# Adding the cross products of a blocked inversion on TensorE, with states and carries copied by ScalarE

## What is computed

```python
def rwkv_scan(state0, r, decay, k, v, a_neg, b, reverse, emit):
    def step(S, inp):
        r_t, w_t, k_t, v_t, a_t, b_t = inp
        sa = einsum('bhij,bhj->bhi', S, a_t)
        S = S * w_t[:, :, None, :] + sa[..., None] * b_t[:, :, None, :] + v_t[..., None] * k_t[:, :, None, :]
        y = einsum('bhij,bhj->bhi', S, r_t) if emit else None
        return S, y
    S, ys = lax.scan(step, state0, xs, reverse=reverse)
```

## Time and profile before

| | |
|---|---|
| runs, median | 1128.56 us (1125.03 to 1128.92, three runs) |
| profiled execution | 1121.17 us, span 1119.4 us |
| busy | TensorE 95%, weight loads 68%, VectorE 61%, ScalarE 35%, GpSimd 30% |
| chain that ended last | TensorE 79%, VectorE 13%, ScalarE 3%, DMA 2%, issue 2% |
| mean granted TensorE clock | 0.980 of full speed |

### The profile page before, as it was taken

The page is one execution under the profiler, slowest core; times in us unless marked ns, Lnnn a source line. Parts: engine busy times, 40 slices in busy tenths (PEclk is TensorE's granted clock), DMA queues, the critical chain, the costliest instruction groups (busy, mean ns, idle before and its releaser), DMA issues.

```text
span 1119.4 us, 17999 instructions
## 1 busy us (share of the span) xinstructions
PE 1063.4 (95%) x7147; PEld 765.1 (68%) x7147; DVE 685.8 (61%) x1456; ACT 396.8 (35%) x1000; POOL 341.4 (30%) x246
## 2 busy tenths in 40 slices
PE   4999999998897897999999999999999999999998
PEld 2544858766786585647559999844656469999743
DVE  3222315586998985697536555698696356555755
ACT  2212213675654141634223444310535114444200
POOL 0000100220021011162027888600251037888400
PEclk9999999998898898999999999999999999999999
DMA  9922342000002302734237544533642244554430
GB/s 354 317 76 76 136 150 80 1 1 1 2 2 86 114 23 76 259 117 151 76 101 231 168 152 163 210 117 112 226 143 83 76 151 151 165 188 176 153 111 37
DMA packets 96981, 140.22 MB, mean 125 GB/s; under 512 B 12255, under 2 KB 63106, under 8 KB 96770
## 3 DMA queue, kind: packets, MB, share of 16 engines
q1 hardware_dynamic: 96532, 138.94, 36.5%
q10 hardware_dynamic: 366, 0.13, 0.0%
HBM read 138.01 MB, written 1.05 MB: 124 GB/s over the span
## 4 chain that ended last, share of the span: by engine, by line
PE 79%; DVE 13%; ACT 3%; DMA 2%; issue 2%; SPq 0%; POOL 0%; DVEq 0%; ACTq 0%
PE bank L1420 22%; PE bank L1460 12%; PE bank L883 10%; PE bank L1231 8%; PE bank L1222 3%; PE bank L499 2%; PE bank L492 2%; DMA ring<-in_ada_w 2%; PE bank L1092 1%; PE bank L1265 1%; PE bank L1163 1%; PE bank L556 1%; PE bank L509 1%; DVE ring L2367 1%; PE bank L680 1%
## 5 line engine op out<-in xcount | busy, mean ns | idle before, releaser
L3089 POOL TENSOR_TENSOR small<-small,con 128x8 f32<-128x8 f32 (+4 forms) x23 | 32.5, 1418 | 423.1 <-DVE small L2741 130.7
L883 PE MATMUL bank<-work,ring 128*128 128x256 f32 (+1 forms) x368 | 118.4, 479 | 0.0
L883 PEld LDWEIGHTS bank<-work,ring 128*128 128x128 f32 x368 | 70.0, 193 | 44.0 <-issue 38.5
L2970 DVE SCALAR_TENSOR_TENSOR bank<-work,prm,bank 128x256 f32<-128x256 f32 x176 | 76.8, 482 | 1.1 <-ACT bank L2030 1.0
L1231 PE MATMUL bank<-ring,work 128*128 128x512 f32 (+1 forms) x192 | 71.7, 526 | 0.0
L2014 ACT ACTIVATE work<-bank 128x128 f32<-128x128 f32 x120 | 33.2, 276 | 103.2 <-PE bank L1420 100.6
L1420 PE MATMUL bank<-xc,work 128*128 128x128 f32 x512 | 65.9, 275 | 2.0 <-ACT work L2014 2.0
L1420 PE MATMUL bank<-work 128*128 128x128 f32 x512 | 65.7, 275 | 0.0
L1420 PEld LDWEIGHTS bank<-xc,work 128*128 128x128 f32 x512 | 61.5, 192 | 2.5 <-ACT work L2014 2.4
L1420 PEld LDWEIGHTS bank<-work 128*128 128x128 f32 x512 | 61.4, 192 | 0.0
L1420 PE MATMUL bank<-work,ring 128*128 128x128 f32 x448 | 59.2, 275 | 0.0
(11 more groups left out here) (526 smaller groups left out, 2291.3 us busy)
## 6 DMA issues: line engine op xcount, KB each, us to landing
ring<-in_w_up SPq DMA_DIRECT2D x32, 1024.0 KB, 7.7
ring<-in_w_in SPq DMA_DIRECT2D x24, 1024.0 KB, 9.1
ring<-in_w_down SPq DMA_DIRECT2D x16, 1024.0 KB, 6.1
ring<-in_ada_w SPq DMA_DIRECT2D x12, 1024.0 KB, 10.5
work<-in_w_up SPq DMA_DIRECT2D x12, 1024.0 KB, 7.0
ring<-in_w_out SPq DMA_DIRECT2D x10, 1024.0 KB, 7.4
work<-in_w_in SPq DMA_DIRECT2D x4, 1024.0 KB, 9.2
work<-in_w_down SPq DMA_DIRECT2D x4, 1024.0 KB, 6.2
```

Source lines behind the costliest of these rows:

```text
L883: ins = mm(b[0:rows, 0:toks], wt[:, k, off:off + rows], hT[:, k, 0:toks], start=(k == 0), stop=(k == KD - 1))
L2970: ins = STT(out=c, in0=hp[:, m % 2, half, tap:tap + SEQ], scalar=k2(l, "conv01", 1, 44 * tap + FB * half + m), in1=c, op0=MUL, op1=ADD)
L3089: return G.tensor_tensor(out_, in_, C("negpow", 1, rows).to_broadcast([rows, n]), POW)
```

## The change

For instances 0 to 3 the addition of the cross products moves from VectorE into PSUM. TensorE first multiplies the other half's right sides by an identity of 64 x 64 into the bank (two products of 512 columns, one per direction), waits on its own semaphore `cross_base` until they have landed, and then lets the eight cross products accumulate on them. ScalarE copies the sum to SBUF as it copies the other stages. `take_carry(2)` and `(3)`: TensorE adds the identity in PSUM, by one more product of 64 columns per head, and ScalarE copies the result. `take_state(0)` to `(3)`: VectorE only makes the gain, at steps 8, 10, 12 and 14; ScalarE copies the state, scaled, in four instructions of 64 columns each. All of VectorE's other asides in the second inversion go. Instances 4 to 7 keep VectorE's versions.

```diff
--- before.py
+++ after.py
@@ -177,6 +177,7 @@
 SEMAPHORES = """a_bar_sc act_T cc_zero column_sums first_consts hT_even hT_odd ssq_ctx angle angle_raw b_spread a_made bk_ch block_T bonus_in c0 c_masked cv_made c_silu c_tanh consts crow d_bias d_hat
  d_rstd d_var d_w decays derived dt_exp e_made ends g_tanh gelu_in gelu_tanh h0 hp_pads k_tok kk_rn kk_sq kkf
  lam_exp lam_sum lora lw_in k_rate maps_used m_bias mix_gmlp mix_rw mix_ssm mod_cols off_made off_step out_done p2_load pads pair_used
+ cross_base state_gain
  up_products up_copies up_corner x_sums weight_sums weight_step early_sums late_row_sums conv_made gelu_square
  params_1 params_2 q_tok qk_rot qk_rstd qk_sum qk_taken qk_turned qk_var r_ch r_grown rk_used rotated rotated_used row_sums rstd_1 rstd_f rstd_lat scale_a scanned row_inv
  sine ssq ssq_a ssq_f t64_diag turns_abs t_inv tables u_theta us v_centred var_1 var_a var_f vec_step vg_n vg_rstd vg_var weights_used
@@ -786,6 +787,12 @@
                     pe.wait_ge(*when_empty(("cross", i, g)))
                 pe.wait_ge(*turn((stage, i, g)))
                 b = bank_of((stage, i, g))
+                added = stage == "cross" and p == 0
+                if added:
+                    for d in range(2):
+                        rows = slice(64 * (1 - d), 64 * (1 - d) + 64)
+                        mm(b[rows, :], ident[rows, rows], factor(2 * i + d)[rows, 4 * g:4 * g + 4, :].rearrange("p a b -> p (a b)"), start=True, stop=False, skip_group_check=True).then_inc(S["cross_base"], 1)
+                    pe.wait_ge(S["cross_base"], 4 * i + 2 * g + 2)
                 for j in range(4):
                     m = 4 * g + j
                     for d in range(2):
@@ -796,7 +803,7 @@
                         if stage == "first":
                             ins = mm(b[one:one + 64, cols], t64[one:one + 64, inst, :], x[one:one + 64, :], start=True, stop=True)
                         elif stage == "cross":
-                            ins = mm(b[two:two + 64, cols], offs[p][one:one + 64, il, m, 32:96], x[one:one + 64, :], start=True, stop=True)
+                            ins = mm(b[two:two + 64, cols], offs[p][one:one + 64, il, m, 32:96], x[one:one + 64, :], start=not added, stop=True, skip_group_check=True)
                         else:
                             ins = mm(b[two:two + 64, cols], t64[two:two + 64, inst, :], x[two:two + 64, :], start=True, stop=True)
                 ins.then_inc(*filling((stage, i, g)))
@@ -813,7 +820,10 @@
                     b = bank_of(("carry", n))
                     for m in SIDES:
                         h, lo = head(m), 64 * (m // 4)
-                        ins = mm(b[lo:lo + 64, 64 * (m % 4):64 * (m % 4) + 64], x[:, m, 0:64], b_tok(n)[:, 64 * h:64 * h + 64], start=True, stop=True)
+                        o = b[lo:lo + 64, 64 * (m % 4):64 * (m % 4) + 64]
+                        ins = mm(o, x[:, m, 0:64], b_tok(n)[:, 64 * h:64 * h + 64], start=True, stop=(i > 1))
+                        if i == 1:
+                            ins = mm(o, ident[:, lo:lo + 64], ident[:, lo:lo + 64], start=False, stop=True)
                     ins.then_inc(*filling(("carry", n)))
                 pe.wait_ge(*turn(("st", n)))
                 b = bank_of(("st", n))
@@ -1793,16 +1803,35 @@
                     tanh_rows(n + 2)
                     key_rates(n + 2)
                 take_keyed_values(n)
-            for stage in ("first", "last"):
+            for stage in ("first", "cross", "last"):
                 for i in range(2):
                     for g in range(2):
                         take_solved(stage, i, g)
+
+            def take_state(n):
+                d = n % 2
+                act.wait_ge(S["state_gain"], n + 1)
+                act.wait_ge(*when_full(("st", n)))
+                b = bank_of(("st", n))
+                for j in range(4):
+                    ins = A.activation(state[:, d, j, :], b[:, 64 * j:64 * j + 64], ACT.Copy, scale=small[:, 288 + 4 * n + j:289 + 4 * n + j])
+                ins.then_inc(*emptying(("st", n)))
+
+            def take_carry(n):
+                act.wait_ge(*when_full(("carry", n)))
+                A.activation(carry[:, n % 2].rearrange("p j n -> p (j n)"), bank_of(("carry", n))[:, 0:256], ACT.Copy).then_inc(*emptying(("carry", n)))
+            take_state(0)
+            take_state(1)
+            take_carry(2)
+            take_carry(3)
             def take_early(j, t):
                 act.wait_ge(*when_full(("early", j, t)))
                 b = bank_of(("early", j, t))
                 A.activation(early_out[:, 2 * j + t, :], b[:, :], ACT.Copy).then_inc(*emptying(("early", j, t)))
             take_early(0, 0)
             take_early(0, 1)
+            take_state(2)
+            take_state(3)
             take_early(1, 0)
 
             def state_times(l):
@@ -2406,9 +2435,12 @@
                 b = bank_of(key)[:, 0:256].rearrange("p (j n) -> p j n", j=4)
                 TT(carry[:, n % 2], b, rep(C("ident64", 64), 4), ADD).then_inc(*emptying(key))
 
+            def state_gain(n):
+                return small[:, 288 + 4 * n:292 + 4 * n]
+
             def take_state(n):
                 d = n % 2
-                gain = small[:, 288 + 4 * n:292 + 4 * n]
+                gain = state_gain(n)
                 vec.wait_ge(S["ends"], n + 3)
                 TT(gain, outward(n), inward(n + 2), MUL).then_inc(S["vec_step"], 1)
                 vec.wait_ge(S["vec_step"], next(vec_steps))
@@ -2636,14 +2668,9 @@
 
             def states_between(step):
                 if step in (8, 10, 12, 14):
-                    q = (8, 10, 12, 14).index(step)
-                    add_cross(q // 2, q % 2)
-                if step in (27, 29):
-                    take_state((step - 27) // 2)
-                if step in (31, 33):
-                    take_carry(2 + (step - 31) // 2)
-                if step in (37, 38):
-                    take_state(step - 35)
+                    n = (8, 10, 12, 14).index(step)
+                    vec.wait_ge(S["ends"], n + 3)
+                    TT(state_gain(n), outward(n), inward(n + 2), MUL).then_inc(S["state_gain"], 1)
             invert(1, states_between)
             for k in range(RB):
                 ins = STT(out=bon[:, k, :], in0=kds[:, k, :], scalar=col("rk", 1, k), in1=rb[:, k, :], op0=MUL, op1=MUL)
```

## The result

The changed kernel takes 1119.47 us in the median of 18 runs (1113.25 to 1126.19), the kernel before 1127.01 us in 18 runs beside it. The ratio, taken over all runs, is 0.9943, with a 95% interval from 0.9922 to 0.9963: 6.4 us less, with an interval from 4.2 to 8.8 (the two medians alone lie 7.5 us apart). The forecast was 4.1 us less (0.9963), 1124.4 us in a range from 1119.5 to 1130.0. It was counted from the median of the first three runs, 1128.56; the ratio times that is 1122.1 us, inside the range, while the median of the 18 runs, 1119.47, stands right at its lower edge. A difference within 0.5% had been given 0.69 and a gain above that 0.24; the measured 0.57% is just on the side of the 0.24, and its interval covers both.

The account below looks back on a forecast made before the run. TensorE's queue was taken to bound the second join, VectorE level within 0.5 us. Projection 2.5 us earlier plus 1.6 us from full clock gave 4.1 us less: 1124.4 us, range 1119.5 to 1130.

Parts of the forecast that it names:

- The bound: At the second join TensorE's queue and VectorE's chain are level within 0.5 us, TensorE the later.
- the wait for state 0: Before the early projection TensorE waits 2.33 us for VectorE's `take_state(0)`, whose state sits in the projection's first PSUM bank.
- The cross stage: Cross solves of instances 0 to 3 on TensorE: 1.92 us each, issued by 364.04, lasts by 367.4.
- cross solve = 0.83 + 0.26 + 0.83: On TensorE: identity pair 0.83 us, wait for its own result 0.26, cross products 0.83; together 1.92.
- The bound below: In the cross stage an identity pair costs TensorE at least 0.83 us, since columns can't be skipped.
- ScalarE: Last copies end at 370.35; states take 0.31 us per 64 columns and leave their banks before the projection wants them.
- The projection: The early projection starts at 374.1 instead of 376.64; its first 16 rows take 7.1 us at full clock.
- The two terms of the sum: At the projection: 2.5 us from its earlier start and 1.6 us from full clock, together 4.1 us.
- The clock did not fall in the solves: Rival: eight short stops in the solves make the clock fall from the second cross on, 8.8 us slower, 1137.4; chance 0.06.
- The pairs overlap: Rival: identity pairs in the cross stage don't overlap, 3.3 us more, gain only 0.8 us, 1127.8; chance 0.13.
- The clock did not fall under the projection: Rival: the clock falls under the projection anyway, leaving only the earlier start, 2.5 us, 1126.1; chance 0.13.
- The rival of a larger gain: TensorE's own waits cost 0.05 us and the 0.94 us stop inside L769 vanishes: gain 5.8 us, 1122.8; chance 0.18.

Follow-up runs that it names:

- the two halves of the change: Kernel before with only states and carries moved to ScalarE, ratios 0.9914 and 0.9933; or with only cross products moved to TensorE and ScalarE, 0.9942.
- the run with the pairs ahead: Changed kernel with the identity products of each cross solve issued one solve ahead: first solve to second join 33.97 us, ratio 0.9952 to the kernel before.
- the kernel's other form: Kernel before, unchanged, in a third profiled execution: 40.39 us from first solve to second join, where the first two executions took 39.61 and 39.60.
- after, timed: Changed kernel, unchanged, timed a second time beside the kernel before: ratio 0.9940, 35.24 us from first solve to second join.
- states only: Kernel before with states and carries of instances 0 to 3 on ScalarE, cross products still added by VectorE: ratio 0.9914, timed once more 0.9933.

## Why the prediction was right, point by point

**The bound.** TensorE's queue and VectorE's chain level at the join, TensorE the later, and the wait for state 0 as the stop to remove: shown, by the two halves of the change, each of which removes it and gains the whole. That VectorE's time alone counts for nothing was right for the whole change: it is done 5.0 us before the join (forecast 4.9), after 30.21 us (forecast 30.6). With states and carries only, where VectorE keeps its adds, it was the later by 0.91 us.

**The cross stage.** Forecast 1.92 us a solve; the rows run at 1.67 (353.18 to 354.85). The step that erred is "cross solve = 0.83 + 0.26 + 0.83". The wait for its own result is real: 1.13 us from an identity pair's start to its cross products, less 0.88 for the pair, is 0.25, as the tail of 0.26 had it. (The Trainium skill, "TensorE: Matmul & The Clock Gate", section "Single matmul latency", gives about 166 ns over the columns' time for a single bf16 product at full clock; that is 0.08 us less than measured here.) But the next pair starts 0.50 us after the cross products do, beside them. The bound below that I gave a pair, 0.83 "since columns can't be skipped", was wrong: beside a cross solve a pair costs almost nothing, as the run with the pairs ahead shows. A pair that stands alone costs 0.88. A small slip stands in the price of a solve: nine solves from 353.04 to 360.67 less the tail are 0.82 us each, not 0.83. The lasts so began 10.18 us after the first solve where the sum had 11.0, and most of this was lost again: ScalarE's copies let 0.4 us of it through, and the last eight groups of the propagations took 3.90 us (365.49 to 369.39) for 3.7.

**ScalarE.** The last copy ended 16.88 us after the first solve (forecast 17.3), the scaled states took 0.21 us an instruction where I had bounded them by 0.31, and no bank was late. As forecast, TensorE waited for the copies before `propagate(2)`.

**The projection.** It starts after 20.88 us (forecast 21.1) and takes 7.07 (forecast 7.1). The two terms of the sum measured 2.72 and 1.66 us where 2.5 and 1.6 were forecast: 4.38 for 4.1. Against the kernel's other form it is 5.2.

**The rivals.** The clock did not fall in the solves, in three executions of three. (The Trainium skill, the same page, section "A second HAM failure mode: psum-queue depth-cycling", warns that micro-idles between groups of products can make the clock swing. At waits of 0.25 us it did not here.) That rival speaks of eight stops; the change has four waits. And the reading of the clock counts three waits ahead of the first fall in the earlier trace rows, but the solve at 363.77 already took 1.54 us, so only the stops of 0.69 and 1.32 us stood ahead of it. The pairs overlap. The clock did not fall under the projection. The rival of a larger gain was right in its size, not in its reasons: it supposed waits of almost nothing, and they cost 0.25 us, and it supposed the stop inside L770 gone, which stayed (1.37, 1.36 and 0.84 us against 0.94, 0.96 and 1.26).

**What stays open.** Runs give 6.4 and 6.8 us, the stretch 4.4 to 5.2. The profiles show where whole executions differ outside the stretch, in work that the change does not touch:

| profile | first solve starts | clock, 255 to 270 us | stretch | second solves to the end |
|---|---|---|---|---|
| before | 353.04 | 0.66 | 39.61 | 720.2 |
| before, again | 354.73 | 0.66 | 39.60 | 720.2 |
| before, third | 354.81 | 0.66 | 40.39 | 725.4 |
| after | 348.51 | 1.00 | 35.23 | 720.8 |
| after, again | 350.16 | 1.00 | 35.23 | 720.5 |
| after, timed | 348.79 | 1.00 | 35.24 | 726.4 |
| states only | 350.43 | 1.00 | 35.46 | 720.6 |
| states only, again | 354.74 | 0.66 | 35.43 | 720.4 |

The first place is the granted clock behind 255 us. TensorE waits there 2.9 us for ScalarE (L1771 before, L1781 after) in every one of them. In the three profiles before the clock is at half behind that wait for some 9 us, in the three after it stays full, and the two profiles of states only, one and the same kernel, have one of each; they are apart by 4.3 us. These two in a longer stretch:

```profile
256.00:300.00 44.00, 39.43 (x406) 31.87 (x406) 38.44 (x75) 28.31 (x69) 0.00 (x0) 1.00 0.01 1
256.00:300.00 44.00, 40.70 (x253) 32.28 (x255) 33.98 (x68) 23.83 (x57) 0.00 (x0) 0.88 0.00 1
```

The second place is behind 420 us, where TensorE waits 1.5 to 2.5 us before two solves for VectorE's reads. In some executions, of either kernel, the low clock lasts through the gate products and what follows them, and 5 to 6 us more go. The changed kernel's first profile and the one beside the second timing:

```profile
400.00:440.00 40.00, 31.41 (x424) 25.42 (x421) 26.11 (x64) 8.86 (x12) 6.95 (x3) 0.91 0.17 54
400.00:440.00 40.00, 33.13 (x402) 27.14 (x400) 21.80 (x58) 5.33 (x9) 6.95 (x3) 0.74 0.16 54
```

So the scatter of whole executions is in good part the clock in these two places, and a pair of profiles may show 10 us that the change did not make. Whether the changed kernel meets the good outcomes more often than the kernel before, which would explain the 2 us between the runs and the stretch, can't be told from three profiles each: at the first place it was three against none, and with the same order of work ahead of it the states-only kernel had both. Part of the rest may also be that the kernel before has still longer forms of the stretch. Two ratios suggest that the runs gain more than the stretch, but do not prove it: the 4.0 us of the usual form (0.9964) lie just outside both intervals, the 5.2 us of the other form (0.9954) inside both. Where the rest comes from is not shown.

## What to carry to other kernels

When two engines are level at a point, look for the wait that one makes for a buffer which the other holds in the middle of a long chain; here moving that one release off the chain was worth the whole gain, however much busy time was moved with it, and a second move for the same wait was worth nothing. An accumulation in PSUM took over an add at almost no price once the identity product was issued ahead of the work that it runs beside, in other quarters of the array. When an engine is relieved in the middle of a fixed order, look at what it meets next: here the relief turned into a wait of 11.56 us at its next instruction, until the order was rewritten. And before a profile is set against another, compare the clock outside the stretch that was changed.

## What I had not expected of the hardware

- Products of 64 rows and 64 columns in different quarters of the array ran four at a time: identity (512 columns) and cross products (128 columns) of two directions started within 0.02 us of each other, and four pairs with four solves (the start of L782 at 356.88 to the first last at 361.17) took 4.3 us where they took 6.6 with a wait between.
- Stops of 0.68, 1.33 and 1.30 us stood in one execution before solves at full clock, and stops of 0.69, 1.32 and 0.85 us in two others before solves that slid to half. Behind one wait of 2.91 us for ScalarE, the same kernel (states only) went on at full clock in one execution (four records of L630 in 0.63 us) and at half in the other (1.09 us). The same stops, then, do not decide the granted clock; a single profile shows one outcome of it.
- The stretch repeated to 0.01 us between executions with the same clock, while whole executions of one kernel lay 13 us apart (1113.25 to 1126.19).
